# Two norms at the edges of a transformer block, by halves: means inside the products beside them, the first half's norm ahead of the last product, one wait moved

## The reference, cut to what matters

```python
h = modulate(rms_norm(x, g_pre_ff1), sh1, sc1)
x = x + 0.5 * ga1 * rms_norm(swiglu(h, w1_gate, w1_up, w1_down), g_post_ff1)   # post norm, residual
h = modulate(rms_norm(x, g_pre_mix), sh2, sc2)                                 # pre norm of the mixer
proj = h @ w_in                                                                # q, k, v and u
attn, ssm = sliding_window_attention(q, k, v), s5_ssm(u, ...)
mixed = concat(rms_norm(attn, g_attn), rms_norm(ssm, g_ssm)) @ w_out
x = x + ga2 * rms_norm(mixed, g_post_mix)
h = modulate(rms_norm(x, g_pre_ff2), sh3, sc3)
x = x + 0.5 * ga3 * rms_norm(swiglu(h, w2_gate, w2_up, w2_down), g_post_ff2)
```

## Time and profile before

| | |
|---|---|
| time, median of 3 | 3109.56 us (3106.25 to 3109.91) |
| the profiled execution: time | 3109.98 us |
| its span (first to last instruction) | 3108.2 us |
| TensorE busy | 96% |
| VectorE, ScalarE, GpSimd busy | 56%, 33%, 7% |
| mean granted TensorE clock | 0.982 of full |
| moved by DMA | 302.5 MB |

### The profile page before, as it was taken

One profiled execution on the slowest core, in us unless ns is written; L12 is line 12 of the kernel. 1 busy time (PEld: TensorE's weight loads), 2 busy tenths in 40 slices (PEclk: granted clock), 3 DMA queues, 4 the chain that ended last, 5 costly groups with the idle time before them and its releaser, 6 DMA issues. The chain is left out here.

```text
span 3108.2 us, 52839 instructions
## 1 busy us (share of the span) xinstructions
PE 2998.5 (96%) x22158; PEld 2606.3 (84%) x22158; DVE 1739.0 (56%) x3387; ACT 1017.0 (33%) x1791; POOL 217.2 (7%) x446
## 2 busy tenths in 40 slices
PE   8999999999999999989999999999999999899998
PEld 7877998999999987789998888878888865688887
DVE  4564577547656346557755765657447444643334
ACT  4655232232112236532323222233222214532222
POOL 0130222000000000211210000000000000000000
PEclk9999999999999999999999999999999999999999
DMA  5201111235433331111224453423324411213232
GB/s 184 103 29 35 52 64 57 75 137 170 161 112 128 113 112 42 41 44 61 69 70 144 161 175 125 158 74 95 115 96 152 153 45 38 82 48 103 88 103 79
DMA packets 75587, 302.54 MB, mean 97 GB/s; under 512 B 10792, under 2 KB 13224, under 8 KB 70360
## 3 DMA queue, kind: packets, MB, share of 16 engines
q1 hardware_dynamic: 58968, 230.04, 22.7%
q0 software_dynamic: 16384, 69.13, 6.2%
HBM read 288.51 MB, written 14.63 MB: 98 GB/s over the span
## 5 line engine op out<-in xcount | busy, mean ns | idle before, releaser
L1126 PE MATMUL acc<-normed_r,toep_r 128*128 128x512 f32 (+2 forms) x1808 | 627.4, 347 | 0.0
L1846 ACT ACTIVATE toep_r<-ring 128x1024 fp32r<-128x1024 f32 (+2 forms) x336 | 388.3, 1157 | 651.4 <-PE acc L1127 620.3
L2385 DVE TENSOR_TENSOR ring_r<-ring,toep_r 128x1024 fp32r<-128x1024 f32 (+2 forms) x336 | 452.8, 1349 | 257.1 <-ACT toep_r L1846 256.8
L1126 PEld LDWEIGHTS acc<-normed_r,toep_r 128*128 128x128 f32 x1808 | 340.2, 188 | 43.1 <-issue 0.2
L1125 PE MATMUL acc<-work_r,toep_r 128*128 128x512 f32 (+2 forms) x1076 | 357.3, 332 | 3.7 <-DVE ring_r L2385 3.6
L1127 PE MATMUL acc<-work_r,ring_r 128*128 128x512 f32 (+2 forms) x1076 | 355.7, 331 | 0.0
L1125 PE MATMUL acc<-mixed_r,toep_r 128*128 128x264 f32 (+1 forms) x1056 | 342.7, 325 | 0.7 <-DVE normed_r L2368 0.6
L1127 PE MATMUL acc<-mixed_r,ring_r 128*128 128x264 f32 (+1 forms) x1056 | 338.8, 321 | 0.0
L1126 PE MATMUL acc<-work_r,toep_r 128*128 128x512 f32 (+2 forms) x968 | 322.2, 333 | 0.0
L1499 PE MATMUL acc<-residual_r,toep_r 128*128 128x264 f32 (+1 forms) x1024 | 301.5, 294 | 3.7 <-ACT toep L2105 2.1
L1125 PE MATMUL acc<-temps_r,toep_r 128*128 128x512 f32 (+1 forms) x752 | 289.6, 385 | 8.2 <-DVE normed_r L2371 4.1
(11 more groups left out here) (448 smaller groups left out, 5415.9 us busy)
## 6 DMA issues: line engine op xcount, KB each, us to landing
ring<-in_w_pair SPq DMA_DIRECT2D x172, 512.0 KB, 3.5
ring<-in_w_down SPq DMA_DIRECT2D x64, 704.0 KB, 4.0
ring<-in_w_gb SPq DMA_DIRECT2D x64, 640.0 KB, 3.9
extra<-in_w_ada POOLq DMA_DIRECT2D x18, 1024.0 KB, 6.0
toep<-in_w_ada POOLq DMA_DIRECT2D x18, 1024.0 KB, 5.9
ring<-in_w_tm SPq DMA_DIRECT2D x24, 512.0 KB, 4.5
ring<-in_w_out SPq DMA_DIRECT2D x24, 512.0 KB, 3.5
ring<-in_w_fm SPq DMA_DIRECT2D x20, 512.0 KB, 4.0
```

The lines of the kernel that those rows point to most:

```text
L1126: mm(out, wh, xl[:, a:z], start=False, stop=False)
L1846: A(high(ld), slot(ld), ACT.Copy).then_inc(S["w_high"], 1)
L2385: V.tensor_tensor(low(ld), slot(ld), high(ld), ALU.subtract).then_inc(S["w_low"], 1)
```

## The change

1. `TILES_AT` becomes earlier: tiles 0 and 1 of the first half are added (VectorE) and squared (ScalarE) ahead of entry 8, tiles 2 to 4 behind it, 5 to 7 behind entry 9. This holds for all three edges (VectorE), and for the two with a pre norm (ScalarE).
2. The first half's tile means: 0 and 1 in the middle of product 9, 2 and 3 behind it, 4 and 5 in the middle of product 10, 6 and 7 behind it. Both edges now have the same order.
3. The first half's norm is cut in two (FRONT): the root and four tiles stand ahead of product 11's values on VectorE and ScalarE, the other four behind.
4. The second half's post mean moves from behind product 11 into the next stage (behind four input tiles of `inputs_lin`'s first job, behind two tiles in `first_lin`), and the second half's eight tile means stand in pairs among the first half's products.
5. The pre norms use PSUM bank 7, so that their sums don't meet the post norms' in bank 6.
6. The wait for the stores moves from ahead of the edge to entry 4.

```diff
-TILES_AT = {KT: (0, 1, 2), KT + 1: (3, 4, 5), KT + 2: (6, 7)}
+TILES_AHEAD, TILES_AT = {KT: (0, 1)}, {KT: (2, 3, 4), KT + 1: (5, 6, 7)}
+MEANS_IN, MEANS_AFTER = {KT + 1: (0, 1), KT + 2: (4, 5)}, {KT + 1: (2, 3), KT + 2: (6, 7)}
+FRONT = range(0, 4), range(4, KT)
...
-                    e["pre"].append(norm(H, e["post"][-1]["done"], range(KT), [span]))
+                    e["pre"].append(norm(H, e["post"][-1]["done"], range(KT), [span], bank=7))
...
-            def edge_lin(e, from_=0, tiles=(), means=None):
+            def edge_lin(e, from_=0, tiles=()):
+                def inside(i):
+                    if i == KT:
+                        post_mean(e, 0)
+                    elif e["pre"]:
+                        pre_means(e["pre"][0], MEANS_IN.get(i, ()))
                 for i, j in enumerate(e["js"]):
                     if i >= from_:
-                        split_lin(j, tiles if i == 0 else (), (lambda: post_mean(e, 0)) if i == KT else None)
-                    for k in (means or {}).get(i, ()):
-                        mean_tile(e["pre"][0], k)
-                post_mean(e, 1)
+                        split_lin(j, tiles if i == 0 else (), (lambda: inside(i)) if i >= KT else None)
+                    if e["pre"]:
+                        pre_means(e["pre"][0], MEANS_AFTER.get(i, ()))
+                if not e["pre"]:
+                    post_mean(e, 1)
...
                 for half, x in enumerate(xs):          # first_lin
-                    if half:
-                        mean_square(then)
...
+                        if half == 0 and k == 1:
+                            post_mean(e, 1)
+                        if half == 0 and 3 <= k < 7:
+                            pre_means(e["pre"][1], range(2 * k - 6, 2 * k - 4))
...
                 for half, (a, z) in enumerate(SPANS):  # inputs_lin
-                    if half:
-                        mean_square(then)
...
+                            if half == 0 and c == 0 and k == 3:
+                                post_mean(e, 1)
+                            if half == 0 and c in (1, 2) and k in (3, 7):
+                                m = 4 * (c - 1) + 2 * (k == 7)
+                                pre_means(e["pre"][1], range(m, m + 2))
...
                 for i, (k, a, z) in enumerate(ENTRIES):   # edge_squares, ScalarE
...
+                        if stored and i == NFULL:
+                            for c in range(2):
+                                act.wait_ge(ssm_stored[c], 8 * 3 * STEP)
                         high_weights(e["lds"][i + 2])
...
+                    if e["pre"]:
+                        for m in TILES_AHEAD.get(i, ()):
+                            square(e["pre"][0], m)
+                        if i == len(ENTRIES) - 1:
+                            root(e["pre"][0])
+                            front(FRONT[0])
...
+                if e["pre"]:
+                    front(FRONT[1])
                 edge_root(e, 1)
...
                 for i, (k, a, z) in enumerate(ENTRIES):   # edge_values, VectorE
+                    added(e["post"][0], g, TILES_AHEAD.get(i, ()))
+                    if front is not None and i == len(ENTRIES) - 1:
+                        front(FRONT[0])
                     total(i - 1)
                     full(dve, e["js"][i])
...
+                    added(e["post"][0], g, TILES_AT.get(i, ()))
+                if front is not None:
+                    front(FRONT[1])
...
+                def normed_part(n, g, at, split=None):
+                    if at[0] == 0:
+                        rinv(n)
+                    normed_tiles(n, g, U, at)
+                    if split is not None:
+                        for k in at:
+                            low_tile(split, k)
```

More of the change, by code:

```diff
@@ L1206, in post_mean @@
                 a, z = SPANS[half]
-                pe.wait_ge(S["mean_read"], n["n"])
+                pe.wait_ge(S["mean_read"], e["post"][0]["n"] + half)
                 pe.wait_ge(S["half_sum"], NSUM * e["n"] + (NSUM if half else 6))
@@ L1277, in ffn @@
                     if half and "edge" in f:
-                        edge_lin(f["edge"], 0, ready, means)
+                        edge_lin(f["edge"], 0, ready)
                         continue
@@ L1693, in second_block @@
             def second_block():
-                ffn(b2["ffn1"], ssm=True, means={KT + 1: range(4), KT + 2: range(4, KT)})
+                ffn(b2["ffn1"], ssm=True)
                 pe.wait_ge(S["bt_staged"], 2 * STEP)
-                inputs_lin(b2["u"], b2["ffn1"]["edge"]["pre"][1])
+                inputs_lin(b2["u"], b2["ffn1"]["edge"])
                 wait(pe, b2["u"][-1].freed)
@@ L1703, in second_block @@
                 halves_lin(b2["out"][0:2], b2["x_out"])
-                edge_lin(b2["mix"], 2, means={KT + 1: range(2), KT + 2: range(2, 5), KT + 3: range(5, KT)})
-                first_lin(b2["ffn2"]["first"], b2["x2"], b2["mix"]["pre"][1])
+                edge_lin(b2["mix"], 2)
+                first_lin(b2["ffn2"]["first"], b2["x2"], b2["mix"])
                 ffn(b2["ffn2"])
@@ L1896, in edge_root, with edge_squares @@
                 A(x, x, ACT.Exp, scale=-0.5).then_inc(S["mean_read"], 1)
-            def edge_squares(e, more=(), root_first=False):
+            def edge_squares(e, more=(), front=None, stored=False):
                 for i, (k, a, z) in enumerate(ENTRIES):
@@ L1919, in edge_squares, with shifted @@
                             square(e["pre"][0], m)
-                if e["pre"] and not root_first:
-                    root(e["pre"][0])
+                if e["pre"]:
+                    front(FRONT[1])
                 edge_root(e, 1)
+            def shifted(half, at):
+                n, (a, z) = b2["ffn1"]["edge"]["pre"][half], SPANS[half]
+                for k in at:
+                    wait(act, n["done"][k])
+                    x = U[:, k, a:z]
+                    A(x, x, ACT.Identity, bias=mod[:, 24 + k:25 + k]).then_inc(S["u_shifted"], 1)
             def ffn(f, then=None, ssm=False):
@@ L1950, in ffn @@
                     if half and "edge" in f:
-                        if ssm:
-                            for s in range(2):
-                                act.wait_ge(ssm_stored[s], 8 * 3 * STEP)
-                        edge_squares(f["edge"], root_first=ssm)
+                        edge_squares(f["edge"], front=(lambda at: shifted(0, at)) if ssm else None, stored=ssm)
                         continue
@@ L2254, in first_block @@
                 ffn(b2["ffn1"], ssm=True)
-                for half, n in enumerate(b2["ffn1"]["edge"]["pre"]):
-                    if half:
-                        squares(n)
-                    a, z = SPANS[half]
-                    for k in range(KT):
-                        wait(act, n["done"][k])
-                        x = U[:, k, a:z]
-                        A(x, x, ACT.Identity, bias=mod[:, 24 + k:25 + k]).then_inc(S["u_shifted"], 1)
+                squares(b2["ffn1"]["edge"]["pre"][1])
+                shifted(1, range(KT))
                 for i, j in enumerate(b2["u"]):
@@ L2299, in first_block @@
                     high_tile(b2["x_out"], k)
-                edge_squares(b2["mix"], b2["first"])
-                high_tiles(b2["x2"][0])
+                edge_squares(b2["mix"], b2["first"], front=lambda at: [high_tile(b2["x2"][0], k) for k in at])
                 squares(b2["mix"]["pre"][1])
@@ L2392, in added @@
             def added(n, g, at):
-                a, z = rinv(n)
+                if at:
+                    a, z = rinv(n)
                 for i in at:
@@ L2399, in added, with edge_values @@
                     V.tensor_tensor(h, h, y, ALU.add).then_inc(S["h_done"], 1)
-            def edge_values(e, g, plus, more=()):
+            def edge_values(e, g, plus, more=(), front=None):
                 def total(i):
@@ L2434, in joint_weights, with ffn @@
                 V.tensor_scalar(LASTW, mean[D], weight[:, KT - 1:KT], None, ALU.mult).then_inc(S["weights_made"], 1)
-            def ffn(f, then, ada=None, l=0, ssm=False, weighted=None):
+            def ffn(f, then, ada=None, l=0, ssm=False, weighted=None, front=None):
                 if f["scaled"]:
@@ L2481, in ffn @@
                     if i >= FH and "edge" in f:
-                        edge_values(f["edge"], then, True)
+                        edge_values(f["edge"], then, True, front=front)
                         continue
@@ L3180, in first_block @@
                     low_tile(b2["x_out"], k)
-                e = b2["mix"]
-                edge_values(e, fg(3), False, b2["first"])
-                normed(e["pre"][0], fg(4), U, split=b2["x2"][0])
-                added(e["post"][1], fg(3), range(KT))
-                normed(e["pre"][1], fg(4), U, split=b2["x2"][1])
+                m = b2["mix"]
+                edge_values(m, fg(3), False, b2["first"],
+                            front=lambda at: normed_part(m["pre"][0], fg(4), at, b2["x2"][0]))
```

(2 more changed lines are left out.)

20 lines of the change are left out of this document (9 added, 11 removed).

## The result

The changed kernel takes 3087.96 us (median of 4 runs, 3085.99 to 3090.10), the kernel before beside it 3107.90 (4 runs, 3103.81 to 3109.91): a ratio of 0.9931, interval 0.9919 to 0.9943. The profiled executions lie 1.6 and 2.1 us above these medians: 3089.53 us with a span of 3087.7 after, 3109.98 with 3108.2 before, 20.5 us of span between them. Forecast were 17.7 us and 3091.9, range 3088.5 to 3098.

What follows compares the result with a forecast made beforehand. TensorE, busy 96%, was taken as the bound. Moved wait 2.2, first edge 9.3 and mix edge 6.2 sum to 17.7 us, taking the median from 3109.56 to 3091.9, range 3088.5 to 3098.

Steps and rivals of the forecast that it cites:

- returns from a mean to a product: TensorE going back from a mean to a product costs some 0.1 us: four in first edge 0.4, nine in mix 1.0.
- What bounds the kernel: TensorE, busy 96% of the span; with no product removed, only its waiting or lower-clock time can come back.
- The moved wait: At product 2, waiting for the stores at entry 4 removes TensorE's stand: 2.2 us, between 1.5 and 2.3.
- The first edge: End of product 9 to second half of inputs_lin: 39.3 us becomes 30.0, no wait left; saves 9.3, bounds 7.9 to 9.7.
- The mix edge: End of product 9 to second half of first_lin: 35.6 us less 25.8 work and 3.55 waits; saves 6.2, bounds 3.5 to 9.8.
- the five waits: Mix edge, TensorE: mean 1, head of first_lin, its third job, second mean of the second half, second half's start; together 3.55 us.
- more goes than I count: Whole kernel: the bounds' other ends are reached, saving 21.8 us, to 3088; chance 0.02.
- Rival A: Clock falls again in the mix half (1.4 to 2.7 us) or both halves (4.1); 3093.3 to 3096; chance 0.20.
- The rule of the Trainium skill: Short idle gaps between matmul groups can make the clock fall repeatedly; by it the mix edge would keep its 0.78.
- Rival B: Add, square and mean chains don't keep up; half of 32 means wait 0.3 us, 4.8 less saved: 3096.7; chance 0.10.
- C: Long low clock in both edges' work without long product runs; slower by over 0.2% from 24 us, at most 3180; chance 0.02.
- D: Waits aren't removed, as early releases meet a queue, such as late reloads before the state space: 3101 or 3107; chance 0.06.

Runs made afterwards that it cites:

- first-edge kernel: The changed kernel with the new order only in the first feed-forward's edge, old order elsewhere and old wait place: 3097.96 us, ratio 0.9965 to the kernel before.
- filler kernel: The kernel before plus four unread products of constants behind the second half's post mean in the first and mix edges: 3107.85 us, ratio 0.9993.
- E1: Not a run but a trace stretch: first edge's post mean in product 8 to the state space's first product; 60.96 us before, 50.88 in the changed kernel.
- E2: Not a run but a trace stretch: mix edge's post mean in product 8 to the next feed-forward's first product; 53.77 us before, 46.83 in the changed kernel.
- its repetition: The unaltered changed kernel measured once more beside the kernel before, on the same chip in five rounds: 3087.99 us, ratio 0.9930.
- two tiles: The changed kernel with two tiles of the norm ahead of product 11's values instead of four, in both edges: 3089.41 us, ratio 0.9928.
- the last kernel: The changed kernel with two norm tiles ahead in the mix edge (four in the first) and tile means 4 to 7 earlier in first_lin: 3085.47 us, ratio 0.9918.
- the mix edge alone: The changed kernel with the new order only in the mix edge, old order elsewhere and old wait place: 3102.99 us, ratio 0.9978 to the kernel before.
- kernel with block means: The changed kernel with the second half's eight tile means in one block ahead of that half, in both edges: 3098.06 us, ratio 0.9961.
- W: Not a run but a trace stretch: VectorE's last hidden values ahead of the first edge to its post mean in product 8; 49.91 us before, 47.40 after.

## Why the prediction was right, and where it fell short

The waits went where the prediction said they would. The step that failed is a term of the sum: the "returns from a mean to a product", put at 0.4 us in the first edge and 1.0 in the mix edge, cost nothing. Next to it stand smaller terms and luck, told one by one here.

- **What bounds the kernel** was right: no product was taken away, and all that came back is TensorE's idle time (13.4 us) and low clock or stretched rows (7.1 us).
- **The moved wait**, forecast 2.2, measured 2.51 in after and again with that part alone. Mechanism right, term mis-sized: I took the bracket, 2.23. Before, the product ahead starts at 2415.99, so at the pitch of 0.23 the next was due at 2416.22 and came at 2418.60, 2.38 later, and the second after it came 0.31 on instead of 0.23. That makes 2.46. The bracket counts from the modelled end of a product, which lies behind its pitch.
- **The first edge**, forecast 9.3, measured 10.08. No wait was left, as worked out. From the end of product 9 to the second half the new order was given 30.0 us; it takes 29.3 (2456.33 less two means of 0.43 is 2455.48, the second half begins at 2484.8). What is too much in the sum is the 0.4 for four returns from a mean to a product. From 2453.35 to 2456.33 in after are 2.98 us: two means, 0.85, and 18 product instructions at 0.118, 2.12. Nothing is left for the return. I had read the 0.1 from a mean that had waited itself, 2460.07 in the earlier trace rows, and the restart after an idle gap looked like a price of the switch. The other 0.3 are rounding in the pitches (16 means at 0.4265, 64 instructions and the rest in 18.1).
- **Between the edges**, forecast nothing, measured 0.88. Before, the clock fell at the start of the attention's output product, on busy TensorE; in after it fell earlier, in the attention's tail, where TensorE stood waiting for part of the time (2.83 busy of 4.00 us) or had one slow mean to make. Windows of before, then of after:

```profile
2658.50:2661.70 3.20, 3.15 (x5) 1.40 (x6) 2.55 (x5) 1.56 (x3) 0.00 (x0) 0.62 0.00 0
2661.70:2672.50 10.80, 10.80 (x46) 8.66 (x46) 5.20 (x9) 3.85 (x6) 0.00 (x0) 0.95 0.00 0
```

```profile
2638.00:2642.00 4.00, 2.83 (x20) 2.09 (x20) 0.59 (x1) 3.12 (x7) 0.00 (x0) 0.54 0.01 4
2642.00:2645.50 3.50, 3.44 (x4) 0.95 (x4) 2.95 (x5) 1.11 (x4) 0.00 (x0) 0.54 0.01 2
```

  The twelve traces have 184.7 to 186.9 in this stretch, which no kernel here changes. In the five long ones (186.6 and over) the last fall begins some 147 us behind the stretch's start, in the seven others (185.9 and less) none does; both kinds have kernels with and without each part of the change. The 0.88 lies inside that spread: it goes with where a fall lands, and no run shows that the change decides it.
- **The mix edge**, forecast 6.2, measured 6.94. The nine returns, 1.0, cost nothing, by the same reading error. Against that the five waits cost a little more than worked out. By pitch they are 0.38, 0.59, 1.12, 0.34 and 1.49, in sum 3.92 (forecast 0.2, 0.4, 1.25, 0.25 and 1.45, in sum 3.55); the brackets of the second, third and fifth say 0.36, 0.86 and 1.25, each some 0.25 too little, as at product 2. 1.0 less 0.37 is 0.6 of the 0.74. Not all of the 6.94 is there in every execution: before lost 2.7 to its fall in the first half, and the 51.29 of the first-edge kernel, which has the own bank and a shorter fall (some 1.5), shows that 1.3 is the bank's and some 2.9 the new order's.
- **The sum**, by the two traces. 0.3 + 0.8 + 0.9 + 0.7 = 2.7 of the 2.8 us over the forecast: 1.4 for the returns, 0.3 for a bracket read as a delay, 0.9 by where a fall landed, less 0.4 for the waits, and some 0.5 of small roundings.
- **The range.** It ended at 3088.5 because I gave "more goes than I count" 0.02. The range had a fall in the new order as a loss, and no fall that a removed gap takes with it: at product 2 the old order falls in two of four traces (before and the filler kernel have none, the other two have one), 1.6 us each. For that the low end should have lain some 1.6 us lower. The 1.4 us of returns too rested on a single row, and the range took them in only as a case of 0.02. That the time came to lie outside, by 0.5 us, is in part luck: the forecast started from 3109.56, the median of three runs of before, and the four runs beside the changed kernel have 3107.90; from there the same 17.7 us give 3090.2, with a low end at 3086.8. Medians of more runs of before (3110.3, 3110.1 and 3109.34) lie near the first value again; beside the second of them after has 3087.99, which makes 22.1 us.
- **Rival A** is refuted: the stretches E1 and E2 in the new order are in five traces each (E1: after and its repetition, first edge alone, two tiles, the last kernel; E2: the mix edge alone in place of the first) and not one shows a granted clock under 1.00. In the old order E1 has a fall in two of four traces and E2 in four of four. The rule of the Trainium skill, TensorE: Matmul & The Clock Gate, section "A second HAM failure mode: psum-queue depth-cycling", that micro-idles between groups of matmuls make the clock go up and down, would have had the mix half fall again; with its gaps of 0.36 and 0.86 it did not. With gaps of 1.5 us and more the traces agree with it part of the time: 1.50 before the first half of `inputs_lin` brought 0.90 in before and 1.00 with the moved wait alone.
- **Rival B** is refuted in size: means waited among products twice, 0.38 and 0.34, both near the forecast, not 16 times. The prediction named such waits as a sign of being wrong, though its own sum had two of them. **C**: no long low clock; the ratio excludes it. **D**: the state space waits 0.69 for ScalarE in after and in before alike, and for no DMA.
- **How much of E1 was clock.** Before had 60.96 with a fall, the kernel with the moved wait 59.39 without one, in the same order. So of the 10.1 us in E1, 8.5 are waits and block means, and 1.6 are a fall that comes and goes.

## What to carry to other kernels

Cut a reduction over tiles into its steps and put them among the products of the neighbouring stage: the largest part that was taken away by itself, 5.6 us in the two edges and 8.7 with a fall of the clock in each, came from eight means in pairs instead of in one block. How far to run ahead has an optimum of its own in each place: of none, two and four tiles ahead of product 11, four were best where products are long (3.9 us), two where they are short (2.8 us) and the values of that product free a buffer. Give two sums that alternate a PSUM bank each: the shared one cost 1.3 us in the old order of the mix edge. And size a gap from start to start against the pitch of its neighbours, not by the idle time shown.

## What the runs showed of the hardware

- The same short gap is followed by a fall of the granted clock in one trace and not in another, and no run shows what decides it. The first half of `inputs_lin` behind a gap of 1.50: 0.90 before, 1.00 with the moved wait alone. Its second half behind 2.07: 1.00 before, 0.52 for the first 2.1 us in the kernel with block means. The first half of `first_lin` behind 1.98: 0.78 before, 1.00 with the first edge alone. At product 2, gaps of 2.23 and 2.27 without a fall and of 2.31 and 2.37 with one. A fall costs some 1.5 to 2.7 us.
- Taking the gaps away took the falls away: of W, E1 and E2, the old order (the filler kernel counted in) has a fall in 8 of 12 stretches, the new one (W with the moved wait, E1 and E2 as in after, with two tiles ahead or as in the last kernel) in 0 of 18.
- Falls go with most of the spread between executions: the same kernel had spans of 3087.7 and 3092.1 with W, E1 and E2 equal to 0.02 us. Ahead of W the granted clock of the first trace is at half for 85 us and the stretch takes 2401.2 us, in the second for 99 and 2405.5. Stretches cut at fixed instructions repeat to 0.02 us where no fall lies in them, whole times to some 4.
- A change between plain fp32 means and products of rounded parts inside a product costs TensorE nothing (2.98 us for 2 means and 18 instructions, from their pitches 2.97).
- The first rows after an idle gap come some 0.25 us later than the bracket lets one think: 2.46 by starts where the bracket says 2.23, 0.59, 1.12 and 1.49 where it says 0.36, 0.86 and 1.25.
